# A two-block layer on one core: convolutions and gated values read from the products' banks, query norm applied as a row factor

## The reference

```
xn = rmsnorm(x)                                       # per token, 1024 wide
lru_x, lru_gate, q, k, v, qi, ki, wi, gate_a, gate_b = split(xn @ w_in)
ua = causal_dwconv(lru_x, 4 taps)                     # the recurrent branch's convolution
ya = rg_lru(ua) * gelu(lru_gate) @ w_lru_br           # uses softplus(-lambda)
qh = rmsnorm(q per head of 128) * q_norm              # 8 heads
kh = rmsnorm(k per head of 128) * k_norm              # 2 key heads, each for 4 query heads
score = sum_h wi_h * relu(qi_h . ki)                  # picks 64 keys for each query
logits = qh . kh * 128**-0.5 + bias(distance), and -inf where a key is hidden or not picked
yb = softmax(logits) @ v @ w_attn_br
x = x + (sigmoid(gate_a) * ya + sigmoid(gate_b) * yb) @ w_out
up = rmsnorm(x) @ w_up                                # 1024 -> 2 x 3072
x = x + (gelu(causal_dwconv(up[:3072], 3 taps)) * up[3072:]) @ w_down     # feed forward
x = x + sigmoid(rmsnorm(x) @ w_ple_gate) * (p @ w_ple_proj)
```

## Time and profile before

| | us |
|---|---|
| median of 3 runs (1871.27 to 1871.55) | 1871.41 |
| the profiled execution, its own time | 1866.17 |
| its span | 1864.4 |
| TensorE busy, matmuls (share of the span) | 1432.7 (77%) |
| TensorE busy, weight loads | 986.5 (53%) |
| VectorE busy | 560.3 (30%) |
| ScalarE busy | 451.2 (24%) |
| GpSimd busy | 566.4 (30%) |

### The profile page before, as it was taken

How to read it: one execution, slowest core, us unless ns; L and a number is a source line. 1 busy time by engine, 2 the same in 40 slices (tenths; PEclk the granted TensorE clock), 3 DMA queues, 4 the chain that set the end, 5 groups by cost and what they waited for, 6 DMA issues and landing times.

```text
span 1864.4 us, 21403 instructions
## 1 busy us (share of the span) xinstructions
PE 1432.7 (77%) x9194; PEld 986.5 (53%) x9194; DVE 560.3 (30%) x874; ACT 451.2 (24%) x554; POOL 566.4 (30%) x151
## 2 busy tenths in 40 slices
PE   6998887865766567656775667564999689899897
PEld 6898886521332133312331233121899678899785
DVE  1997366000000000000000000002658942257602
ACT  3354531100000000000000000002347353534433
POOL 6786363000000000000000000002384738687782
PEclk9999999988998898889988898888799899899998
DMA  8453338899999999999999999999155333445450
GB/s 325 153 182 136 124 136 315 324 409 410 410 410 410 410 410 410 409 410 410 410 410 410 410 410 410 410 409 393 52 181 204 136 113 136 141 183 185 169 180 23
DMA packets 116576, 539.42 MB, mean 289 GB/s; under 512 B 4440, under 2 KB 8544, under 8 KB 108832
## 3 DMA queue, kind: packets, MB, share of 16 engines
q1 hardware_dynamic: 113232, 532.44, 73.1%
q0 software_dynamic: 1184, 3.94, 0.6%
q10 hardware_dynamic: 2096, 2.11, 0.4%
HBM read 537.41 MB, written 1.06 MB: 289 GB/s over the span
## 4 chain that ended last, share of the span: by engine, by line
DMA 40%; PE 32%; DVE 11%; SPq 7%; ACT 5%; issue 3%; POOL 2%; DVEq 0%; ACTq 0%
DMA ring<-in_w 39%; PE bank L547 26%; SPq L381 7%; PE bank L766 4%; DVE slab L1423 2%; POOL ring_parts L485 2%; ACT ring_parts L1008 2%; DVE slab L1427 1%; DMA ring<-in_units 1%; DVE slab L1508 1%; DVE rows_parts L1755 1%; DVE slab L1849 0%; DVE slab L1486 0%; PE bank L752 0%; DVE slab L1517 0%
## 5 line engine op out<-in xcount | busy, mean ns | idle before, releaser
L485 POOL TENSOR_TENSOR ring_parts<-ring,ring_parts 128x2048 fp32r<-128x2048 f32 x114 | 547.6, 4829 | 259.3 <-ACT ring_parts L1008 259.3
L766 PE MATMUL bank<-ring,slab 128*32 128x512 f32 x2016 | 335.5, 801 | 304.6 <-DMA ring<-in_w 303.7
L547 PE MATMUL bank<-slab_parts,ring_parts 128*128 128x256 f32 x3328 | 506.1, 288 | 27.5 <-DVE slab_parts L1438 14.2
L547 PEld LDWEIGHTS bank<-slab_parts,ring_parts 128*128 128x128 f32 x3328 | 464.9, 196 | 33.6 <-DVE slab_parts L1438 14.8
L766 PEld LDWEIGHTS bank<-ring,slab 128*32 128x32 f32 x2016 | 65.7, 133 | 563.4 <-DMA ring<-in_w 389.9
L499 POOL TENSOR_TENSOR slab_parts<-slab,slab_parts 128x1088 fp32r<-128x1088 f32 x1 | 2.5, 2494 | 946.9 <-ACT slab_parts L1157 946.9
L1008 ACT ACTIVATE ring_parts<-ring 128x2048 fp32r<-128x2048 f32 x114 | 211.6, 1908 | 114.3 <-PE bank L547 114.3
L1689 DVE TENSOR_TENSOR slab<-slab,bank 128x512 f32<-128x512 f32 x16 | 11.0, 687 | 624.4 <-PE bank L766 624.4
L547 PE MATMUL bank<-rows_parts,ring_parts 128*128 128x256 f32 x752 | 188.1, 287 | 0.0
L547 PE MATMUL bank<-ring_parts,slab_parts 128*128 128x512 f32 (+1 forms) x672 | 166.2, 398 | 15.2 <-POOL ring_parts L485 6.5
L547 PEld LDWEIGHTS bank<-ring_parts,slab_parts 128*128 128x128 f32 x672 | 129.8, 196 | 44.4 <-POOL ring_parts L485 8.2
(11 more groups left out here) (290 smaller groups left out, 916.1 us busy)
## 6 DMA issues: line engine op xcount, KB each, us to landing
ring<-in_w SPq DMA_DIRECT2D x190, 2048.0 KB, 23.7
ring<-in_units SPq DMA_DIRECT2D x59, 2048.0 KB, 8.0
slab<-in_w SPq DMA_DIRECT2D x2, 2048.0 KB, 14.9
ring<-in_units SPq DMA_DIRECT2D x2, 1024.0 KB, 14.1
slab<-bias_scratch ACTq DMA_DIRECT2D x2, 1024.0 KB, 8.0
slab<-in_xT SPq DMA_DIRECT2D x1, 1024.0 KB, 5.2
rows<-in_ln_g POOLq DMA_DIRECT2D x2, 512.0 KB, 8.8
slab<-in_x SPq DMA_DIRECT2D x1, 1024.0 KB, 4.9
```

Of the source, the lines that this page charges most:

```text
L485: g.tensor_tensor(r32(w), w, r32(high), ALU.subtract).then_inc(S("low_ready"), 1)
L547: return mm(out_, l, r, start=start and first, stop=stop and last)
L766: last = mm(b[CAP * j:CAP * j + CAP, :], xg[:, c, CAP * j:CAP * j + CAP], wt[:, j, i, :], start=c == 0, stop=c == DC - 1, tile_position=(0 ...
```

## The change

Five things are changed; what is computed stays the same up to rounding.

1. `causal_conv` becomes `bank_conv`: both convolutions read the product's bank itself. ScalarE's copies of the `lx` and `fg` banks are gone, and a bank is read only when its last tap has run.
2. The gated value of the feed forward is made in its bank (`tt(o, o, hj)`); the high part is copied from the bank by ScalarE, one bank at a time, and the low part is the bank less the high part, which then frees the `fu` bank.
3. The query norm becomes a factor of a logit's row. One task `qsum` sums the squares with 16 products of one column each, into 16 columns of a bank; a root, an inverse and a scaling act on 128 x 16 numbers (`q_scale`). The two gains are multiplied into one (`qk_gain`) and put on the keys. The logits wait for the queries' copies and the keys only.
4. A logit bank is scaled and given its bias in place, one instruction for each head, and the mask is added on the way out of the bank, which frees it.
5. The rate of the recurrence is worked out at the very start of the program, ahead of the long convolution, and its exponential ahead of ScalarE's first sigmoid.

The diff has eight columns of indentation taken off, and the block from `glu_input` to `low_turned`, which moves unchanged below the rate's instructions, is left out of it.

```
     n2 += ["kk", "vv", "qi0", "qi1"] + [f"dots{t}_{j}" for t in range(2) for j in range(4)]
     n2 += [f"lr{j}" for j in range(4)] + [f"li{j}" for j in range(4)]
     n2 += ["ksum"] + [f"qq{j}" for j in range(4)]
-    n2 += ["gc0", "gc1"] + [f"qsum{j}" for j in range(4)] + ["gc2", "gc3", "ya0", "ya1"]
+    n2 += ["gc0", "gc1"] + ["qsum"] + ["gc2", "gc3", "ya0", "ya1"]
     for t in range(2):
         n2 += [f"log{t}_{j}" for j in range(4)]
     n2 += ["ya2", "ya3"]
...
 k_sq = slab[:, 8, 1280:1792]
 wih = slab[:, 8, 1792:1808].rearrange("p (t h) -> p t h", t=TT)
 best = slab[:, 8, 1808:1816]
+q_scale = small[:, 0:TT * NH]
+qk_gain = small[:, 144:145]
 rel = [slab[:, s, :] for s in (6, 9)]
 lgt = slab[:, 4, :].rearrange("p (h s) -> p h s", h=NH)
 prob_t = slab[:, 5, :].rearrange("p (s h t) -> p s h t", s=TT, h=NH)
...
             for m in range(2):
                 c = 2 * j + m
                 if x == 0:
-                    pe.wait_ge(S("lru_tap"), 2 * LRU_W * (j + 1))
+                    wait_read(pe, f"lx{j}")
                 last = mm(o[:, T * m:T * m + T], w[:, 8 * x + c, :], chan(2)[:, c, :], start=True, stop=True)
             full(last, f"{pre}{j}")
     o = take_bank("ksum")
...
     chan_major(unit(1), xn, ["qq0", "qq1"])
     chan_major(unit(1), xn, ["qq2", "qq3"])
     chan_major(unit(1), xn, ["gc0", "gc1"])
-    for j in range(4):
-        o = take_bank(f"qsum{j}")
-        pe.wait_ge(S("q_sq_ready"), j + 1)
-        full(mm(o[:, 0:512], ones[:], slab[:, 6, 512 * j:512 * j + 512], start=True, stop=True), f"qsum{j}")
+    o = take_bank("qsum")
+    pe.wait_ge(S("q_sq_ready"), 4)
+    for t in range(TT):
+        for h in range(NH):
+            last = mm(o[:, NH * t + h:NH * t + h + 1], chan(6)[:, h, P * t:P * t + P], ones[:, 0:1],
+                      start=True, stop=True)
+    full(last, "qsum")
     chan_major(unit(1), xn, ["gc2", "gc3"])
     pe.wait_ge(S("lru_low"), 1)
     chan_major(unit(1), lru_parts, ["ya0", "ya1"])
     pe.wait_ge(S("k_ready"), 1)
-    pe.wait_ge(S("q_ready"), 4)
+    wait_read(pe, "qq0", "qq1", "qq2", "qq3")
     for t in range(TT):
         n = P * (t + 1)
         for j in range(4):
...
         o = [take_bank(f"dn{u}_{t}") for t in range(TT)]
         for k in range(3):
             if u == 0:
-                pe.wait_ge(S("hid_low"), 2 * k + 2)
+                wait_read(pe, *[f"fu{2 * k + i}_{j}" for i in range(2) for j in range(2)])
             w = unit(1)
             x = [part[:, DC * k:DC * k + DC, :] for part in hid_parts]
             for t in range(TT):
...
     act.wait_ge(S("xt_landed"), 16)
     A(r32(slab[:, 8, :]), slab[:, 0, :], ACT.Copy).then_inc(S("xt_high"), 1)
     act.wait_ge(S("cols_landed"), 16)
+    act.wait_ge(S("lam_negabs"), 1)
+    A(small[:, 80:88], small[:, 72:80], ACT.Exp).then_inc(S("lam_exp"), 1)
     per_chunk(["g0"], chan(1), ACT.Sigmoid, "b_conv_g")
     weights_high(0, "a1")
     per_chunk(["g1"], chan(1), ACT.Sigmoid, "b_conv_g", first=2)
...
             ins.then_inc(S("xn_high"), 1)
     take_turned([f"x2t{j}" for j in range(4)], "mix_norm")
-    act.wait_ge(S("lam_negabs"), 1)
-    A(small[:, 80:88], small[:, 72:80], ACT.Exp).then_inc(S("lam_exp"), 1)
     weights_high(1, "lx3")
     o = wait_full(act, "kiwi_k")
     read(A(kiT, o[:, 0:T], ACT.Copy), "kiwi_k")
...
         act.dma_start(slab[:, 2, :].rearrange("p (h j) -> p h j", h=NH), src
                       ).then_inc(S("bias_landed"), 16)
-    per_chunk(["lx0", "lx1"], chan(1), ACT.Copy)
-    weights_high(1, "lg_1")
-    per_chunk(["lx2", "lx3"], chan(1), ACT.Copy, first=4)
-    weights_high(1, "lg_3")
+    weights_high(1, "lg_1", "lg_3")
     per_chunk(["lg_0", "lg_1"], chan(3), ACT.Gelu_apprx_tanh)
     weights_high(1, "vv")
     per_chunk(["lg_2", "lg_3"], chan(3), ACT.Gelu_apprx_tanh, first=4)
...
     per_chunk(["gc0", "gc1"], chan(3), ACT.Sigmoid)
     weights_high(1, "ya1")
-    for j in range(4):
-        o = wait_full(act, f"qsum{j}")
-        read(A(slab[:, 6, 512 * j:512 * j + 512], o[:, 0:512], ACT.Sqrt, bias=eps_rms[:], scale=1.0 / HD),
-             f"qsum{j}")
+    o = wait_full(act, "qsum")
+    read(A(q_scale, o[:, 0:TT * NH], ACT.Sqrt, bias=eps_rms[:], scale=1.0 / HD), "qsum")
     per_chunk(["gc2", "gc3"], chan(3), ACT.Sigmoid, first=4)
     weights_high(1, "ya3")
...
     down = ["dn0_1/1", "dn0_1/2", "dn0_1", "dn1_1/1", "dn1_1/2", "dn1_1"]
     for i in range(6):
-        for j in range(2):
-            o = wait_full(act, f"fg{i}_{j}")
-            if i >= 2:
-                act.wait_ge(S("ffn_tap"), 4 * FFN_W * (i - 1))
-            read(A(half(4, i % 2)[:, 2 * j:2 * j + 2, :].rearrange("p a t -> p (a t)"), o[:, 0:512],
-                   ACT.Copy), f"fg{i}_{j}")
         weights_high(1, f"fg{i + 1}_1" if i < 5 else down[0])
-        act.wait_ge(S("ffn_tap"), 4 * FFN_W * (i + 1))
+        wait_read(act, f"fg{i}_0", f"fg{i}_1")
         A(half(5, i % 2), half(5, i % 2), ACT.Gelu_apprx_tanh).then_inc(S("fgelu_ready"), 1)
         weights_high(1, f"fu{i + 1}_1" if i < 5 else down[1])
-        wait_read(act, f"fu{i}_0", f"fu{i}_1")
-        A(r32(hT[:, 4 * i:4 * i + 4, :]), half(5, i % 2), ACT.Copy).then_inc(S("hid_high"), 1)
+        for j in range(2):
+            act.wait_ge(S("hid_made"), 2 * i + j + 1)
+            A(r32(hT[:, 4 * i + 2 * j:4 * i + 2 * j + 2, :].rearrange("p a t -> p (a t)")),
+              bank(f"fu{i}_{j}")[:, 0:512], ACT.Copy).then_inc(S("hid_high"), 1)
     weights_high(1, *down[2:])
     weights_high(1, "pg0_1", "pg1_1")
     for t in range(TT):
...
         dve.wait_ge(S(done), base + n)
         return base + n
-    def causal_conv(src, dst, w, width, bias, chunks, done, base, between=None):
...
+    def bank_conv(tasks, dst, w, width, bias, first, done, base):
+        o = [wait_full(dve, task) for task in tasks]
+        chunks = range(2 * len(tasks))
+        n = base
+        for lag in range(width):
+            for c in chunks:
+                src = o[c // 2][:, T * (c % 2):T * (c % 2) + T]
+                wc = col(w, width * (first + c) + width - 1 - lag)
                 if lag == 0:
-                    ins = ts(dst[:, cd, :], src[:, cs, :], wc, col(bias, cw), ALU.mult, ALU.add)
+                    ins = ts(dst[:, c, :], src, wc, col(bias, first + c), ALU.mult, ALU.add)
                 else:
-                    dve.wait_ge(S(done), base + n - len(chunks) + 1)
-                    ins = stt(dst[:, cd, lag:T], src[:, cs, 0:T - lag], wc, dst[:, cd, lag:T],
-                              ALU.mult, ALU.add)
-                n += 1
-                ins.then_inc(S(done), 1)
-            if between and lag in between:
-                between[lag]()
-        dve.wait_ge(S(done), base + n)
-        return base + n
+                    dve.wait_ge(S(done), base + len(chunks) * (lag - 1) + c + 1)
+                    ins = stt(dst[:, c, lag:T], src[:, 0:T - lag], wc, dst[:, c, lag:T], ALU.mult, ALU.add)
+                if lag == width - 1 and c % 2:
+                    read(ins, tasks[c // 2])
+                else:
+                    ins.then_inc(S(done), 1)
+                    n += 1
+        return n
     def low_part(full_, high, low):
...
     dve.wait_ge(S("cols_landed"), 16)
-    glu_input([0, 1])
...
     lam = cols[:, COLS["lam"]:COLS["lam"] + 8]
     stt(small[:, 72:80], lam, -1.0, lam, ALU.mult, ALU.min).then_inc(S("lam_negabs"), 1)
     dve.wait_ge(S("lam_exp"), 1)
...
     ts(pl, pl, -8.0, None, ALU.mult).then_inc(S("rate_ready"), 1)
+    glu_input([0, 1])
...
-    for j in range(4):
-        wait_read(dve, f"lx{j}")
-        causal_conv(chan(1), chan(2), "lru_w", LRU_W, "lru_b", [(2 * j + m,) * 3 for m in range(2)],
-                    "lru_tap", 2 * LRU_W * j)
+    n = 0
+    for j in range(4):
+        n = bank_conv([f"lx{j}"], chan(2)[:, 2 * j:2 * j + 2, :], "lru_w", LRU_W, "lru_b", 2 * j, "lru_tap", n)
...
     low_part(slab[:, 1, :], slab[:, 5, :], slab[:, 1, :]).then_inc(S("lru_low"), 1)
     wait_read(dve, "ksum")
+    tt(qk_gain, col("k_norm"), col("q_norm"), ALU.mult).then_inc(S("qk_step"), 1)
     v.reciprocal(k_sq, k_sq).then_inc(S("qk_step"), 1)
-    dve.wait_ge(S("qk_step"), 1)
-    stt(slab[:, 7, 0:512], slab[:, 7, 0:512], col("k_norm"), k_sq, ALU.mult, ALU.mult
+    dve.wait_ge(S("qk_step"), 2)
+    stt(slab[:, 7, 0:512], slab[:, 7, 0:512], qk_gain, k_sq, ALU.mult, ALU.mult
         ).then_inc(S("k_ready"), 1)
-    for j in range(4):
-        wait_read(dve, f"qsum{j}")
-        r6 = slab[:, 6, 512 * j:512 * j + 512]
-        q9 = slab[:, 9, 512 * j:512 * j + 512]
-        v.reciprocal(r6, r6).then_inc(S("qk_step"), 1)
-        dve.wait_ge(S("qk_step"), j + 2)
-        stt(q9, q9, col("q_norm"), r6, ALU.mult, ALU.mult).then_inc(S("q_ready"), 1)
+    wait_read(dve, "qsum")
+    v.reciprocal(q_scale, q_scale).then_inc(S("qk_step"), 1)
+    dve.wait_ge(S("qk_step"), 3)
+    ts(q_scale, q_scale, HD ** -0.5, None, ALU.mult).then_inc(S("qk_step"), 1)
+    dve.wait_ge(S("qk_step"), 4)
```

(33 more changed lines are left out.)

59 lines of the change are left out of this document (27 added, 32 removed).

## The result

| | before | after |
|---|---|---|
| median of 4 runs, us | 1871.48 (1871.27 to 1873.95) | 1852.18 (1850.97 to 1852.33) |
| ratio, 95% interval | | 0.9892 (0.9875 to 0.991) |
| the profiled execution, its own time | 1866.17 | 1852.33 |
| its span | 1864.4 | 1850.6 |
| VectorE, ScalarE, GpSimd busy | 560.3, 451.2, 566.4 | 465.9, 440.5, 556.7 |

A forecast was written before the change was run, and what follows sets the result against it. No engine was full throughout; TensorE waited on normed queries before the logits and on GpSimd's low parts at the down products. 9.8 + 1.3 + 5.7 + 2.7 = 19.5 off 1871.4 gave 1851.9 us, range 1847 to 1863.5.

The forecast's parts named there:

- Log products, 9.8 + 1.3: Attention: TensorE's wait for the normed queries before the logits goes, 9.8 us; the 32 instructions at full clock gain 1.3.
- net 0, at worst 1: Tile 1's logits, scaled and biased in place: banks held 1.6 instead of 0.7 us, net 0, at worst 1 us.
- Down products, 5.7 + 2.7: Feed forward's end: an unstalled convolution removes three waits for GpSimd, 5.7 us, and the low clock after them, 2.7.
- Gated value: 0: Feed forward: gated value in place, low part from the bank, gains 0, as the bank is needed only after 23 us.
- qsum, rate, `lx`, copies at 0: Thin square sums (3.6 us, covered by a wait before `ya0`), rate at the start, recurrent convolution without copies: each 0.
- A TENSOR_SCALAR from the bank: Feed forward convolution read from banks: four TENSOR_SCALARs of 0.43 us and eight taps of 0.44, 5.2 us, never stalled.
- The prediction's 0.8 more for the twelve: A block's twelve convolution instructions: PSUM's 120 fixed cycles against 58 and a lost doubled rate, some 0.8 us more, hidden.
- Carrying the 5.2 us: Whole kernel: the profiled execution lay 5.2 us below its runs' median, and the forecast kept that offset, giving 1851.9.
- the rivals: Attention gain given back 0.09, down waits stay 0.10, clock falls 0.08, slower from stalled bank reads 0.04, nothing 0.03.
- Thin products let the clock fall: Rival at qsum: `gc2`, `gc3` and part of `ya0` run at half speed, 3.5 us lost, 1855.4; chance 0.08.

The follow-up runs named there:

- e9: e5 with block 0 of the feed forward (of six) keeping its gated value, high and low part in SBUF as before; 1867.09 us, 1.0002 to before.
- e5: Kernel before with only the gated value made in place, its high and low parts taken from the bank, convolution still from SBUF copies; 1857.14 us, 0.9951.
- e12: Changed kernel with the 32 qsum instructions run twice over (64 of one column); one execution, 1855.98 us.
- e3: Kernel before with only the recurrence's rate moved to the start and the recurrent convolution read from the banks; 1869.73 us, 0.9998.
- e4: Kernel before with the feed forward's convolution reading the banks but still waiting for ScalarE's two unread copies, gated value as before; 1860.64 us, 0.995.
- e7: Changed kernel with the row maximum negated by the reduction itself and the query scale's factor put into the keys' gain; 1846.62 us, 0.9885 to before.
- e10: e7 with ScalarE making the high part of unit gd2/gd3 behind tile 1's exponentials instead of ahead of them; 1849.12 us, 0.9903 to before.
- e8: e7 with ScalarE making the high part of unit ya0/ya1 before it waits for the recurrence's product; 1846.22 us, 0.9885 to before.

## Why the prediction was right, and where its steps were not

- **Log products, 9.8 + 1.3: right.** The wait and the low clock both went (the second gave 1.6). Counted from the start of the attention stretch, TensorE is 11.55 us ahead when the turn of tile 1 starts, and 10.2 when it is over: the turn waits 2.3 us instead of 1.4, and its 16 products take 3.56 us instead of 1.97 at the clock that fell in that wait. The step called "net 0, at worst 1" looked at the banks and at `pv0` (which waits 2.0 instead of 2.7), and not at what a longer wait does to the clock of the turn; it cost 1.4.
- **Down products, 5.7 + 2.7: right in size, the cause incomplete.** 9.3 was measured. The waits went to the last, 5.7; the clock gives back 3.0, not 2.7 (6.0 us at the lower level, shown at e9); the other 0.6 is not accounted for. I read one block, the last, found its convolution stalled, and took that for the cause. It was a link, and the last, of a cascade whose first stall was the low part of block 0.
- **"Gated value: 0" failed.** The step named 1.23 to 5.5 us for the low part, and cleared it because its bank was not wanted for 23 us. What the longer 5.5 does to GpSimd, and GpSimd to the next convolution, was not followed. Alone it is worth 9.4 us (e5); beside the convolution it is worth nothing, and only therefore did the sum hold. That was luck and not foresight.
- **qsum, rate, `lx`, copies at 0: right** (e12, e3, e4). 32 thin products took 3.63 us, forecast 3.6.
- **A TENSOR_SCALAR from the bank took 536 ns, not 430** (in the earlier trace rows: 425 for one that had no column as a scalar, 538 for one that writes a bank); the taps took 474 against the 440 taken. The twelve were 5.0 us with their overlap, forecast 5.2, and 0.5 more than the same twelve unstalled from SBUF. All of the 0.5 is in the TENSOR_SCALARs; the taps took 476 ns from SBUF. The prediction's 0.8 more for the twelve counts the fixed cycles alone, and not the lost doubled rate that it names beside them.
- **Carrying the 5.2 us: right for the median, wrong for the profile.** The profile of after had its own time at its runs' median, since it fell in the other group of starts. That 1851.9 and 1852.18 lie so close is in part luck too: the block gained 19.9, since the turn's loss of 1.4 was more than made up by what came beyond the forecast up to the end of the log products (0.5), in the feed forward (0.9) and behind it (0.4).
- None of the rivals came. "Thin products let the clock fall" exists, at twice their number.

## What to carry to other kernels

When an engine's instruction is many times its usual length, go back block by block to the first that is, and ask what pushed it into the other engine's way; the stall beside the wait may be the end of a chain, and several parts of a change may then each bring the whole gain. Removing a stalled instruction gained nothing while the next GpSimd half lay in the way of its successor (e7); move the other engine's work too (e10). Compare executions by stretches that start at the same instruction.

## What the runs showed of the hardware that was not expected

- VectorE's product of two columns of 128 x 1 took 4.55 us beside GpSimd (e8, L1854), nearly as much as one of 128 x 2048 (4.87), and the scaling of 128 x 16 took 4.33 (after, L1863): here the stall did not shrink with the size, down to one column.
- Half a microsecond between the starts of VectorE and GpSimd decided between 3.24 and 11.96 us for eight taps; GpSimd's four halves took 21.0 us behind VectorE's taps and 18.5 ahead of them.
- 32 products of one column left the clock at 1.00; in a run of 64 it fell to its lower level after 5.0 us, though TensorE was busy without a break.
- A wait of 2.3 us before the turn of tile 1 was followed by 3.56 us for 16 products, one of 1.4 us by 1.97.
